# RWKV recurrence: exchanged partition halves, and a 32x32 inverse with its levels 1 to 4 as a loop on TensorE

## What is computed

```python
def rwkv7_recurrence(r, decay, kk, b, k, v, s0):
    def step(s, inp):
        r_t, w_t, kk_t, b_t, k_t, v_t = inp
        sa = jnp.einsum('dbhvk,dbhk->dbhv', s, kk_t)
        s = s * w_t[..., None, :] - sa[..., :, None] * b_t[..., None, :] + v_t[..., :, None] * k_t[..., None, :]
        return s, jnp.einsum('dbhvk,dbhk->dbhv', s, r_t)
...
    y, s_fin = rwkv7_recurrence(
        both(rh, rh), both(decay_h[:, :, 0], decay_h[:, :, 1]), both(kk, kk),
        both(b_dir[:, :, 0], b_dir[:, :, 1]), both(k_dir[:, :, 0], k_dir[:, :, 1]), both(vh, vh),
        jnp.moveaxis(s0.astype(f32), 1, 0))
    y = y[0] + jnp.flip(y[1], axis=1)
```

## Time and profile before

| | |
|---|---|
| median of three runs | 2690.67 us |
| profiled execution, time of the run | 2691.81 us |
| its span, first to last instruction | 2689.8 us |
| mean granted clock of TensorE | 0.961 |
| the recurrence, first matmul to last `y` | 457.55 to 796.30 us |
| its third tile | 595.93 to 663.74 us |
| GpSimd's share of the span | 8% |

### The profile page before, as it was taken

One profiled execution on the slowest core, in us unless ns is written; L12 is line 12 of the kernel. 1 busy time (PEld: TensorE's weight loads), 2 busy tenths in 40 slices (PEclk: granted clock), 3 DMA queues, 4 the chain that ended last, 5 costly groups with the idle time before them and its releaser, 6 DMA issues.

```text
span 2689.8 us, 74227 instructions
## 1 busy us (share of the span) xinstructions
PE 2448.0 (91%) x34058; PEld 1706.7 (63%) x34058; DVE 601.4 (22%) x1164; ACT 536.0 (20%) x1037; POOL 217.9 (8%) x243
## 2 busy tenths in 40 slices
PE   5899985999999769999999899998794999999998
PEld 3555564999994466777666345457453777766654
DVE  1113456666652330000000010106315000000001
ACT  3111043444421310000000036114413000000000
POOL 2000020333300010000000000003001000000000
PEclk8999997999999889999999999999896999999999
DMA  7665300000012269999999311110014999999970
GB/s 282 191 216 180 132 1 14 4 4 4 4 44 68 108 248 373 397 397 396 396 394 392 115 50 47 48 63 32 16 58 159 353 392 397 396 394 394 396 274 39
DMA packets 173468, 529.19 MB, mean 197 GB/s; under 512 B 23124, under 2 KB 27888, under 8 KB 173296
## 3 DMA queue, kind: packets, MB, share of 16 engines
q1 hardware_dynamic: 158688, 489.45, 48.1%
q10 hardware_dynamic: 10336, 24.21, 3.1%
q0 software_dynamic: 4272, 12.91, 1.4%
HBM read 506.75 MB, written 11.40 MB: 193 GB/s over the span
## 4 chain that ended last, share of the span: by engine, by line
PE 68%; issue 16%; DMA 5%; DVE 3%; ACT 2%; POOLq 1%; ACTq 1%; DVEq 1%; POOL 1%; SPq 0%
PE ps L1710 19%; PE ps L1725 17%; PE ps L1124 7%; PE ps L458 4%; PE ps L1840 4%; DMA big<-w_exp_down 3%; PE ps L1209 2%; PE ps L1912 2%; PE ps L1134 2%; PE ps L1908 2%; PE ps L460 1%; PE ps L830 1%; PE ps L438 1%; PE ps L1703 1%; PE ps L1196 1%
## 5 line engine op out<-in xcount | busy, mean ns | idle before, releaser
L1710 PE MATMUL ps<-rs,ring 128*64 128x80 f32 x12288 | 441.8, 233 | 5.8 <-issue 5.5
L1710 PEld LDWEIGHTS ps<-rs,ring 128*64 128x64 f32 x12288 | 429.9, 137 | 23.9 <-issue 23.0
L1811 DVE TENSOR_TENSOR big<-big,ps 128x320 f32<-128x320 f32 x64 | 28.3, 483 | 993.8 <-PE ps L1725 954.8
L1725 PE MATMUL ps<-big 128*80 128x512 f32 x512 | 226.4, 595 | 1.9 <-DMA big<-w_exp_down 1.5
L1725 PE MATMUL ps<-ring,big 128*80 128x512 f32 x512 | 225.0, 592 | 2.4 <-DVE big L1811 2.4
L555 PE MATMUL ps<-hT,ring 128*128 128x512 f32 x336 | 176.1, 606 | 11.1 <-ACTq L602 11.1
L1124 PE MATMUL ps<-big 64*64 64x64 f32 x5440 | 166.5, 219 | 16.9 <-DVEq L1095 16.9
L1781 ACT COPY big<-ps 80x512 f32<-80x512 f32 x64 | 34.1, 582 | 711.0 <-PE ps L1725 711.0
L1124 PEld LDWEIGHTS ps<-big 64*64 64x64 f32 x5440 | 163.1, 136 | 18.2 <-DVEq L1095 17.2
L1725 PEld LDWEIGHTS ps<-ring,big 128*80 128x80 f32 x512 | 76.6, 150 | 145.9 <-issue 141.8
L1725 PEld LDWEIGHTS ps<-big 128*80 128x80 f32 x512 | 74.3, 150 | 131.5 <-issue 129.8
(11 more groups left out here) (392 smaller groups left out, 3002.1 us busy)
## 6 DMA issues: line engine op xcount, KB each, us to landing
ring<-w_exp_up SPq DMA_DIRECT2D x124, 1024.0 KB, 10.8
ring<-w_exp_gate SPq DMA_DIRECT2D x68, 1024.0 KB, 12.1
big<-w_exp_down SPq DMA_DIRECT2D x64, 1024.0 KB, 11.3
ring<-w_exp_down SPq DMA_DIRECT2D x64, 1024.0 KB, 11.5
big<-w_exp_gate SPq DMA_DIRECT2D x60, 1024.0 KB, 10.6
big<-w_ada SPq DMA_DIRECT2D x22, 2048.0 KB, 8.7
ring<-w_in_odd SPq DMA_DIRECT2D x6, 2048.0 KB, 8.9
big<-big ACTq DMA_DIRECT2D x32, 256.0 KB, 6.4
```

What stands on the lines that cost most here:

```text
L1710: last = nc.tensor.matmul(ps[2 * m + j // 4][a:a + HALF, (j % 4) * SLOTS:(j % 4 + 1) * SLOTS], ex_blocks[ex_slot(q)][:, k % 2, j * P + a:j ...
L1725: last = nc.tensor.matmul(ps[4 + f][0:SLOTS, :], hid[:, k, :], ex_blocks[ex_slot(q)][:, k % 2, f * W:(f + 1) * W], start=(k == 0), stop=(k ...
```

## The change

It has three parts.

- *Exchanged halves.* In every other pair of heads (c = 1 and 3) the results of the two heads change places: what came from the lower half of the partitions is written to the upper, and the reverse. `across` and `added_across` issue the four matmuls of two pairs of heads one after another: lower rows to lower columns, upper to upper, lower to upper and upper to lower, in two banks. `each` stays where both operands are already exchanged (M·V, Phi, Hm). The state, its scales `em` and R have to be put into that place too: `place_em_pe` and `place_em_act` for the scales, a product with the identity for R (`r_turned`, `r_placed`), and matmuls instead of transposes for the states at the start and the end.
- *A 32x32 inverse.* L is kept as quarters: the two diagonal 32x32 blocks of each 64x64 block, and the corner between them. The levels 0 to 4 run on 32x32 blocks (`quarters`: four matmuls of 32x32 on 32 columns for a column of blocks, on the four diagonal places of the array), and level 5 becomes `corner_left` and `corner_right`. On TensorE the levels 1 to 4 are one hardware loop (`pe.Fori`), whose semaphore counts come from a register; ahead of four of the products in it stands one matmul of `quarter_ident` that nothing reads. The two lora groups move ahead of the loop and behind it.
- *The order on VectorE.* `Rst` is made behind level 0 of the same tile instead of at the end of the tile before; the scales and `Sc` are made behind the pairs instead of at the start of the tile. TensorE waits at the start of a tile for `sc_made` (the state read out of its bank) and `em_placed`, no longer for `rwkv_y_kept` behind the first two products only.

The core of the diff:

```diff
+        def place_em_pe(turn, pe):
+            for e in BOTH:
+                pe.wait_ge(sem("exps"), turn * 2 + (e + 1))
+                odd_pairs = em[e].rearrange("p (a f u) -> p f a u", a=2, f=2)[:, 1]
+                for g in range(2):
+                    last = nc.tensor.matmul(ps[4 * e + 1][HALVES[1 - g], 0:4].rearrange("p (a u) -> p a u", a=2), half_ident[HALVES[g], :],
+                                            odd_pairs[HALVES[g]], start=True, stop=True)
+                last.then_inc(sem("em_crossed"), 1)
...
+                def quarters(b, lhs, rhs):
+                    for j in range(RB):
+                        for g in QUARTERS:
+                            last = nc.tensor.matmul(ps[b][g, narrow(j)], lhs[g, j, :], quarter_ident[g, :] if rhs is None else rhs[g, j, :],
+                                                    start=True, stop=True)
+                    return last
...
+                def pair_quarters(e):
+                    for k in range(4):
+                        for f in range(2):
+                            j = 4 * (k // 2) + 2 * f + k % 2
+                            for g in range(2):
+                                for q in range(2):
+                                    nc.tensor.matmul(ps[4 * e + f][QUARTERS[2 * (g ^ f) + q], narrow(k)], Bst[e][HALVES[g], j, QUARTERS[q]],
+                                                     Ast[e][HALVES[g], j, QUARTERS[q]], start=True, stop=True)
...
+                def corner_left(e):
+                    for j in range(RB):
+                        for h in range(2):
+                            last = nc.tensor.matmul(ps[4 * e + 1][QUARTERS[2 * h + 1 - e], narrow(j)], corner[e][QUARTERS[2 * h + e], j, :],
+                                                    X[e][QUARTERS[2 * h + e], j, :], start=True, stop=True)
+                    return last
...
+                def corner_right(e):
+                    for j in range(RB):
+                        for h in range(2):
+                            g = QUARTERS[2 * h + 1 - e]
+                            nc.tensor.matmul(ps[4 * e + 3][QUARTERS[2 * h + e], narrow(j)], T1[e][g, j, :], XT[e][g, j, :], start=True, stop=True)
+                            last = nc.tensor.matmul(ps[4 * e + 3][g, narrow(j)], quarter_ident[g, :], XT[e][g, j, :], start=True, stop=True)
+                    return last
...
+                def across(b, lhs, rhs, apart=1):
+                    for k in range(4):
+                        for f in range(2):
+                            for g in range(2):
+                                last = nc.tensor.matmul(ps[b + apart * f][HALVES[g ^ f], k * N:(k + 1) * N], half_ident[HALVES[g], :] if lhs is None else lhs[f][k][HALVES[g]],
+                                                        half_ident[HALVES[g], :] if rhs is None else rhs[f][k][HALVES[g]], start=True, stop=True)
+                    return last
...
                 pe.wait_ge(sem("tile_ready"), n * 4 + 4)
                 for e in BOTH:
-                    each(4 * e + 1, Bst[e], Ast[e]).then_inc(sem("pairs_done"), 1)
-                for e in BOTH:
-                    turned(4 * e + 2, blocks_of(Ast[e])).then_inc(sem("abk_turned"), 1)
+                    if n:
+                        pe.wait_ge(sem("sc_made"), n * 4 + (e - 1))
+                    pe.wait_ge(sem("em_placed"), n * 2 + (e + 1))
+                    pair_quarters(e).then_inc(sem("pairs_done"), 1)
...
                 for e in BOTH:
                     pe.wait_ge(sem("v_kept"), n * 2 + (e + 1))
+                    across(4 * e + 2, None, r_of[e]).then_inc(sem("r_turned"), 1)
+                for e in BOTH:
+                    pe.wait_ge(sem("r_placed"), n * 2 + (e + 1))
                     each(4 * e + 3, MT[e], Vtok[e]).then_inc(sem("mv_done"), 1)
...
-                for lv in range(1, LEVELS):
+                pe.wait_ge(sem("incl_kept"), n * 4 + 4)
+                if n + 1 < NT:
+                    prepare_lora_pe(n + 1, 0, pe)
+                pe.wait_ge(sem("mv_kept"), n * 2 + 2)
+                with pe.Fori(1, LEVELS - 1) as lv:
                     for e in BOTH:
-                        pe.wait_ge(sem("x_updated"), n * 2 * (LEVELS - 1) + (2 * (lv - 1) + e + 1))
...
+                        pe.wait_ge(sem("x_updated"), lv * 2 + (n * 2 * (LEVELS - 1) + e - 1))
+                        pe.wait_ge(sem("level_masked"), lv * 2 + (n * 2 * (LEVELS - 1) + e + 1))
+                        nc.tensor.matmul(ps[4 * e + 1][0:QN, RB * QN:RB * QN + QN], quarter_ident, quarter_ident, start=True, stop=True)
+                        quarters(4 * e + 1, Lm[e], X[e]).then_inc(sem("lx_done"), 1)
                     for e in BOTH:
-                        if lv == 1:
...
-                            pe.wait_ge(sem("mv_kept"), n * 2 + (e + 1))
-                        pe.wait_ge(sem("lx_kept"), n * 2 * (LEVELS - 1) + (2 * (lv - 1) + e + 1))
...
+                        pe.wait_ge(sem("lx_kept"), lv * 2 + (n * 2 * (LEVELS - 1) + e - 1))
+                        pe.wait_ge(sem("xt_updated"), lv * 2 + (n * 2 * LEVELS + e - 1))
+                        nc.tensor.matmul(ps[4 * e + 2][0:QN, RB * QN:RB * QN + QN], quarter_ident, quarter_ident, start=True, stop=True)
...
+                    for e in BOTH:
+                        quarters(4 * e + 3, T1[e], XT[e]).then_inc(sem("xt_product"), 1)
+                if n + 1 < NT:
+                    pe.wait_ge(sem("a_made"), n * 2 + 3)
+                    prepare_lora_pe(n + 1, 1, pe)
+                for e in BOTH:
+                    pe.wait_ge(sem("x_updated"), n * 2 * (LEVELS - 1) + (2 * (LEVELS - 2) + e + 1))
+                    corner_left(e).then_inc(sem("lx_done"), 1)
+                for e in BOTH:
+                    pe.wait_ge(sem("lx_kept"), n * 2 * (LEVELS - 1) + (2 * (LEVELS - 2) + e + 1))
+                    pe.wait_ge(sem("xt_updated"), n * 2 * LEVELS + (2 * (LEVELS - 2) + e + 1))
+                    corner_right(e).then_inc(sem("xt_product"), 1)
...
+                def added_across(b, k, terms):
+                    for t, (lhs, rhs) in enumerate(terms):
+                        for f in range(2):
+                            for g in range(2):
+                                last = nc.tensor.matmul(ps[b + f][HALVES[g ^ f], k * N:(k + 1) * N], lhs[f][HALVES[g]], rhs[f][HALVES[g]],
+                                                        start=(t == 0), stop=(t == 2))
+                    return last
...
+                    if step and n + 1 < NT:
+                        place_em_pe(n + 1, pe)
                     for e in BOTH:
                         u = 1 - e if step else e
-                        for c in range(RC):
-                            j = 2 * c + u
-                            last = added(4 * e + 3, j, [(Vtok[e][:, j], TkT[e][:, j]), (nWG[e][:, j, N:P], TbT[e][:, j]), (state[e][:, c], Hm[e][:, j])])
+                        for a in range(2):
+                            k = 2 * a + u
+                            last = added_across(4 * e + 2, k, [(two(Vtok[e], k), two(TkT[e], k)), (two(nWG[e][:, :, N:P], k), two(TbT[e], k)),
+                                                               ([state[e][:, 2 * f + a] for f in range(2)], two(Hm[e], k))])
...
-                        nc.vector.tensor_tensor(XT[e], XT[e], bank(4 * e + 3), ALU.subtract).then_inc(sem("xt_updated"), 1)
+                        if lv < LEVELS - 1:
+                            nc.vector.tensor_tensor(XT[e], XT[e], narrow_bank(4 * e + 3), ALU.subtract).then_inc(sem("xt_updated"), 1)
+                        else:
+                            nc.vector.tensor_copy(XTf[e][:, :, QUARTERS[1 - e]], narrow_bank(4 * e + 3)).then_inc(sem("xt_updated"), 1)
...
-                for e in BOTH * more:
-                    prepare_r_dve(n + 1, e, dve)
```

More of the change, by code:

```diff
@@ L48 @@
                       ("rot", P), ("cos", TS), ("sin", TS), ("edges", 2 * P),
[L49 removed]
+                      ("chain", 512), ("strict", 2 * N), ("within", 2 * N), ("level", 2 * (LEVELS - 1) * QN), ("quarter_ident", QN), ("quarter", 2),
                       ("half_ident", N),
@@ L101, in constants @@
     lv = []
-    for h in [2 ** i for i in range(LEVELS)]:
+    s, tt = p[:, None] % QN, np.arange(QN)[None, :]
+    for h in [2 ** i for i in range(LEVELS - 1)]:
         same = s // (2 * h) == tt // (2 * h)
@@ L106, in constants @@
     put("level", np.stack([np.stack(x, 1) for x in lv], 2))
+    put("quarter_ident", s == tt)
+    put("quarter", p[:, None] % N // QN == np.arange(2)[None, :])
     put("half_ident", np.concatenate([np.eye(N), np.eye(N)], 0))
@@ L968, in build @@
         HALVES = (slice(0, N), slice(N, P))
+        QUARTERS = [slice(QN * g, QN * (g + 1)) for g in range(4)]
         def four(x):
@@ L1150, in rwkv_pe @@
+                    quarters(4 * e + 1, Lm[e], None).then_inc(sem("x_product"), 1)
                 for e in BOTH:
                     pe.wait_ge(sem("abk_kept"), n * 6 + (e + 1))
```

(19 more changed lines are left out.)

164 lines of the change are left out of this document (99 added, 65 removed).

## The result

The changed kernel takes 2746.83 us (median of four runs, 2743.96 to 2747.05) against 2690.82: 1.0209 times the time before, 95% interval 1.019 to 1.0228. The forecast was 2626 us, with 0.16 for slower. The profiled execution lasts 2746.76 us; its page begins

The account below looks back on a forecast made before the run. Matmuls on TensorE alone were taken to set the pace. Tile: 13.4 + 24.2 + 8.8 + 8.2 = 54.6 us against 67.81; kernel: 2691.8 - 67.1 + 1.4 = 2626 us, range 2595 to 2692 (about 0.8).

Parts of the forecast that it names:

- What bounds the kernel now: RWKV mixer tiles: TensorE busy 67.79 of 67.81 us, so the matmuls alone set the pace.
- Four places at a time: Array places: four matmuls side by side, 14.6 ns per matmul in `across`, 7.9 in the 32-wide products.
- Pairs, turns, M·V: 13.4 us: First stretch of a tile: 11.9 us of matmuls plus shape changes and waits, 13.4 in place of 18.67 us.
- A trip 4.2 to 4.8 us: Loop over inverse levels: 4.2 us a trip, the fourth 4.8 for ScalarE's exponentials; four trips 17.4 us.
- The branch: Hardware loop of the levels: 0.2 us a trip, taken from at most 0.23 in the loops over experts.
- a change of shape: Changes of matmul tile shape on TensorE: 0.09 us each; if a 0.218 us drain instead, tile 58.5, kernel 2646 us.
- The corner and the second loras: 4.9 us: After the loop: corner 3.0 us including 0.9 of waits, and one of two loras at 1.9 us each.
- W/G and Phi: 8.8: Stretch until the second direction's `phi_kept`: unchanged but for its banks, 8.8 us.
- The last stretch: States and outputs: outputs halve, but the VectorE, ScalarE, GpSimd chain holds the next tile; 8.2 in place of 9.9 us.
- no more matmuls than before: Rival: TensorE's price per instruction decides, from 15 ns; at 26 ns tile 95, kernel 2829 us, slower; chance 0.16.
- The lower clock: Rival: TensorE falls to the lower clock in the loop, same price as nothing gained, 2693 us; chance 0.07 together.
- The signs: Wrong if: 64 `quarters` over 0.9 us, trip above 5.6, clock 0.5 in loop, or issue waits inside straight stretches.

Follow-up runs that it names:

- The exchange alone: Exchanged halves with their products and order, but the earlier kernel's 64x64 inverse, six levels written out; against the kernel before: 2689.49 us, ratio 1.0007.
- the halves not exchanged: Changed kernel with the same instructions and waits, but each group of four matmuls on two array places instead of four: 2743.97 us, 1.0214 against the kernel before.
- the kernel with more code: Kernel before plus 256 unread 32x32 matmuls (512 in the trace) written out at each tile's start: 2760.76 us, ratio 1.0263; as a loop 2729.65, 1.015.

## Why the prediction was wrong, point by point

- *What bounds the kernel now* was read one step short. A TensorE that is busy 67.79 of 67.81 us says that nothing else is later, not by how much the next thing is earlier. The next bound, the packets, lay a tenth behind: 17 of them in the tile, and the forecast did not ask how soon one can follow another. The supply of instructions stands in no term of its sum.
- *Four places at a time* was right: 64 matmuls of `across` in 0.88 us at best (forecast 0.93 for 64), `quarters` at 8.4 to 8.9 ns (7.9). The Trainium skill, TensorE: Matmul & The Clock Gate, section "Wait — 56ns, not 53.3ns?", has 25 ns from start to start as a floor; these rows are below it, across places of the array. The slower time does not come from that floor.
- *Pairs, turns, M·V: 13.4 us* is the step that failed most: 25.50 measured, seven packets at 3.6. The stretch holds 896 matmuls; at 14.6, 7.9 and, for M·V, 29.2 ns they are the 11.9 us of work that were summed (with the other terms 13.3, not 13.4), and the sum left out that each has to arrive. The exchange alone and the halves not exchanged, both of which moved nothing, show it.
- *A trip 4.2 to 4.8 us* is right, or nearly, for the trips that run from code already there (4.61, and 5.00 with a wait of 0.4 for VectorE), and wrong for the first (9.38, three packets) and the second (6.17, at a clock of 0.68 behind the stops). Four trips 25.2 us instead of 17.4. The single matmuls cost 0.32 each where 0.05 + 0.18 were set, 1.4 us a tile of that. The branch, set at 0.2, showed as 0.32 between bare trips and as nothing beside the single matmuls. For what a change of shape costs the forecast weighed 0.09 against a drain of 0.218; 0.32 less the 0.05 of the matmul itself make 0.13 each for in and out, between the two.
- *The corner and the second loras: 4.9 us* were 6.79, with 1.7 us put down to issue. *W/G and Phi: 8.8* were 11.32 at a clock of 0.77. The last stretch, *8.2*, was 8.61: the chain over VectorE, ScalarE and GpSimd was read rightly (GpSimd's second product ends at 694.02, 7.9 us behind `phi_kept`; 8.1 were set), and `place_em_pe` held nothing up. But the chain did not end the stretch: TensorE was still at its outputs, and the next tile's first product came 0.7 us later.
- Together 12.1 + 7.8 + 1.9 + 2.5 + 0.4, and 0.1 of the first loras, are 24.8 us over the forecast's 54.6, and the tile is 79.4.
- *The rivals.* The first, "no more matmuls than before", had the right sign and the right kind of price, one per instruction, 26 ns among its bounds. Its place was wrong: it put the price on every matmul that TensorE hands out, so it charged every trip of the loop and came to 2829. It was argued away with a burst of sixteen matmuls, far inside a packet of 128, which can't show what follows a packet. The lower clock was a rival too; the traces show 0.5 behind some of the stops, in parts of the pairs, the first two trips, the corner and W/G. How much of the 24.8 us it costs by itself was not separated: the second trip is 1.6 us longer than the fourth, and W/G and Phi 2.5 longer than forecast. Against its being the main cause stands the exchange alone, which gained nothing in pairs at 1.00.
- *The signs.* Of those that the prediction named for being wrong, three came: waits put down to issue inside straight stretches, trips above 5.6 us (9.38 and 6.17), and a clock of 0.5 in the loop. The first of them points at the cause.

The Trainium skill, Runtime: NRT & Kernel Launch, section Instruction fetch mechanics, says that code comes in blocks of 16 KB ahead of execution and that crossing a block is mostly hidden. The trace has the blocks; hidden they are only while 128 matmuls last longer than 3.3 to 3.6 us. The section also prefers unrolling to branches; here the kernel with its loop written out is 94 us slower.

## What to carry to other kernels

Ahead of making an engine's instructions cheaper, count them against the rate at which they arrive: here 128 small matmuls every 3.3 to 3.6 us in straight code, on the queue of instructions that the page lists. Near that rate, what helped here was fewer instructions (one load for two products) or code that runs again from a loop, which needed no packets from its second trip on. Where the array's places set the pace, as in the 64x64 levels, the loop gained nothing, and its single matmuls cost 26 us. A fully busy engine is not proof that it is the only bound; look for the one just behind it.

## What the runs showed that was not expected

- The 49 KB of the loop's body (392 matmuls, three packets) ran three more trips without a single packet: from 652.24 to 668.02 the instruction queue is empty in the changed kernel.
- Stops for packets can bring a clock of 0.50 behind them: in the kernel with more code the clock read 0.65 on the mean over its 512 matmuls (625.14 to 636.85), and 1.00 where the same ran as a loop. Stops alone do not: the pairs of the exchange alone have five, the longest 1.9 us, and stay at 1.00. What makes the difference was not found out.
- 64 matmuls of 64x64 on 128 columns at four places start within 1.65 us at best, 26 ns each, at the pace of the packets: a form in which neither the array nor the packets wait for the other.
